# A hybrid encoder block with 16,384 single-neuron experts: the first-table tiles of its dense part shared out anew over the steps and begun three steps earlier

## The reference

```python
def block(xb):                      # 128 tokens
    q = (xb @ w_q).reshape(128, 8, 2, 128)          # 8 heads, two halves
    s1 = einsum('thd,hkd->thk', q[:, :, 0], k1)     # 128 keys each
    s2 = einsum('thd,hkd->thk', q[:, :, 1], k2)
    v1, i1 = top_k(s1, 16);  v2, i2 = top_k(s2, 16)
    cand_s = v1[..., :, None] + v2[..., None, :]
    cand_i = i1[..., :, None] * 128 + i2[..., None, :]
    top_s, pos = top_k(cand_s, 16)                  # 16 experts of 16,384
    idx = take_along_axis(cand_i, pos)
    gate = softmax(top_s)
    u = expert_u[idx];  vv = expert_v[idx]          # a row of 1,024 each
    act = gelu(einsum('td,thkd->thk', xb, u))
    return einsum('thk,thkd->td', gate * act, vv)
x = layer_norm(alpha * x + block(x))
```

## Time and profile before

| | before |
|---|---|
| median of 3 runs | 3006.27 us (3006.0 to 3010.39) |
| the profiled execution | 3014.1 us, its span 3012.3 us |
| TensorE's mean granted clock | 0.921 of full speed |
| TensorE busy | 2616.7 us, 87% |
| VectorE busy | 2327.7 us, 77% |
| ScalarE busy | 1223.7 us, 41% |
| GpSimd busy | 971.8 us, 32% |
| DMA | 1100.76 MB, mean 365 GB/s |

### The profile page before, as it was taken

The page is one execution under the profiler, slowest core; times in us unless marked ns, Lnnn a source line. Parts: engine busy times, 40 slices in busy tenths (PEclk is TensorE's granted clock), DMA queues, the critical chain, the costliest instruction groups (busy, mean ns, idle before and its releaser), DMA issues. The chain is left out here.

```text
span 3012.3 us, 53462 instructions
## 1 busy us (share of the span) xinstructions
PE 2616.7 (87%) x20618; PEld 1518.2 (50%) x20618; DVE 2327.7 (77%) x4875; ACT 1223.7 (41%) x3048; POOL 971.8 (32%) x888
## 2 busy tenths in 40 slices
PE   9899978787887767768888869999998997999997
PEld 7677433232332333323333326666676775766774
DVE  7965577999879899976767867767788884877776
ACT  3254143233345555533333423333244332544454
POOL 0000144444445555544343522223232222211221
PEclk9999999889997777779998989999999999999998
DMA  4113699999999999999999989999999999999995
GB/s 165 63 56 140 240 403 419 413 404 417 412 419 405 420 411 420 419 420 421 421 418 406 419 336 383 397 394 401 400 416 375 397 412 411 386 392 369 410 393 210
DMA packets 175382, 1100.76 MB, mean 365 GB/s; under 512 B 17829, under 2 KB 34341, under 8 KB 52778
## 3 DMA queue, kind: packets, MB, share of 16 engines
q0 software_dynamic: 110592, 805.36, 65.3%
q1 hardware_dynamic: 64554, 292.16, 24.5%
HBM read 1061.79 MB, written 35.65 MB: 364 GB/s over the span
## 5 line engine op out<-in xcount | busy, mean ns | idle before, releaser
L975 POOL DMA_INDIRECT arena_high<-uv_dram,idx_now x768 | 929.3, 1210 | 1665.9 <-PE ps L1258 1525.2
L2430 DVE SCALAR_TENSOR_TENSOR arena_high<-arena_low,arena_high 128x1024 f32<-128x1024 f32 x768 | 922.4, 1223 | 267.4 <-DMA arena_high<-uv_dram,idx_now 261.5
L1258 PE MATMUL ps<-arena_high 32*32 32x512 f32 x12288 | 493.5, 671 | 282.5 <-ACT arena_high L1815 278.1
L1496 PE MATMUL ps<-arena_low 128*128 128x256 f32 x2048 | 463.7, 382 | 0.0
L1496 PEld LDWEIGHTS ps<-arena_low 128*128 128x128 f32 x2048 | 384.0, 190 | 109.4 <-issue 46.0
L1806 ACT ACTIVATE gcol<-hcol 128x2 f32<-128x2 f32 x384 | 77.6, 202 | 824.4 <-DVE arena_high L2430 820.0
L1258 PEld LDWEIGHTS ps<-arena_high 32*32 32x32 f32 x12288 | 94.8, 107 | 481.6 <-ACT arena_high L1815 384.6
L1219 PE MATMUL ps<-arena_low 128*128 128x512 f32 (+1 forms) x512 | 242.0, 616 | 14.3 <-DMA arena_low<-slabs_dram 14.3
L332 PE MATMUL ps<-wv_hi_bytes,w_hi_bytes 128*128 128x512 f32 x512 | 207.6, 406 | 19.4 <-DVE v_lo_bytes L2554 13.1
L1815 ACT ACTIVATE arena_high<-arena_high,wcol 128x32 f32<-128x32 f32 x768 | 204.9, 314 | 12.5
L334 PE MATMUL ps<-wv_hi_bytes,w_lo_bytes 128*128 128x512 f32 x512 | 202.3, 395 | 0.0
(11 more groups left out here) (264 smaller groups left out, 4002.4 us busy)
## 6 DMA issues: line engine op xcount, KB each, us to landing
arena_low<-ut_dram SPq DMA_DIRECT2D x64, 1024.0 KB
arena_high<-vt_dram SPq DMA_DIRECT2D x32, 1024.0 KB, 12.7
arena_low<-vt_dram SPq DMA_DIRECT2D x32, 1024.0 KB
arena_low<-spread_dram SPq DMA_DIRECT2D x32, 512.0 KB
acts_dram<-arena_low SPq DMA_DIRECT2D x14, 1024.0 KB
arena_low<-acts_dram SPq DMA_DIRECT2D x28, 512.0 KB
arena_low<-slabs_dram SPq DMA_DIRECT2D x11, 1152.0 KB
arena_high<-uv_dram,idx_now POOLq DMA_INDIRECT x768
```

Of the source, the lines that this page charges most:

```text
L975: pool.indirect_dma_start(out=ring[:, s % RING, :], out_offset=None, in_=uv_d, in_offset=bass.IndirectOffsetOnAxis(ap=idx_now[:, s:s + 1], ...
L1258: last = nc.tensor.matmul(ps[out:out + QUAD, y_bank(t // PH) + turn, :], diag[rows, s % DIAGS, :], ring[rows, s % RING, cs], start=fresh, ...
L1496: last = nc.tensor.matmul(ps[:, 5 + n % 4 // 2, o:o + 2 * P], u_slot[n % USLOTS][:, k, :], x1T[:, BLK - DENSE:BLK, k, :], start=(k == 0), ...
L2430: last = nc.vector.scalar_tensor_tensor(out=ring[:, s % RING, 0:D], in0=x1[c][:, j, :], scalar=1.0, in1=ring[:, s % RING, 0:D], op0=ALU.mu ...
```

## The change

Four things are altered; what is computed stays the same.

1. *Start of the first table.* It begins three steps earlier (`U0` = 253, step 5 of turn 31). For that slab 12 goes by `beside_u` too: both halves of its queries in bank 4, a quarter in each of steps 1, 2, 4 and 5 of turn 31 (the code shifts them one step ahead of the later slabs' pattern), its scores in step 7, in banks 7 and 4. The first tile now waits for slab 12's scores, not slab 13's. SyncE issues slab 13 before the third tile pair, the one that waits for `y_read`.
2. *Shares.* `u_first` goes by weights: 133 for the steps up to turn 38, 193 for those of turn 39 and after the groups, 95 for the steps with gate groups. Tiles of turns 31 to 43 were 0, 10, 11, 11, 11, 11, 11, 11, 11, 11, 10, 11, 9 and are 3, 11, 10, 11, 10, 11, 10, 11, 15, 8, 8, 12, 8.
3. *Gate groups.* On 18 steps (21, 21, 22 groups in turns 40 to 42 become 24, 29, 11), beginning at G = 321; VectorE builds the one-hot tiles one step ahead in four buffers; in a step TensorE and ScalarE do the groups before the tiles. The picks are still turned round at G = 320.
4. *Second table.* 29 steps in place of 31, from G = 348; 7 steps of experts alone behind it in place of 3. The loads of the gates for the first two chunks are issued at tile 124, ahead of the last pair of first-table loads, not after it. Tiles of turns 43 to 47 were 8, 33, 33, 33, 21 and are 17, 35, 36, 35, 5.

```diff
-U0 = 32 * STEPS
-TAIL = 3
-V_STEPS = 31
+U0 = 32 * STEPS - 3
+TAIL = 7
+V_STEPS = 29
...
-G_STEP0 = PICK0 + DENSE * PH * PICK_PARTS - U0
-G_STEPS = 24
+G_STEP0 = PICK0 + DENSE * PH * PICK_PARTS - U0 + 1
+G_STEPS = 18
+HOTS = 4
+G_BACK = G_STEP0 + G_STEPS + 4
...
+def u_share(s):
+    G = U0 + s
+    if G < PICK0 + 7 * STEPS:
+        return 133
+    return 95 if G_STEP0 <= s < G_STEP0 + G_STEPS else 193
 def u_first(s):
-    return NT * s // U_STEPS
+    return NT * sum(u_share(i) for i in range(s)) // sum(u_share(i) for i in range(U_STEPS))
...
-        hot = at(16, 2, 4, 2 * P)
+        hot = [at(kib, 4, 2 * P) for kib in (16, 20, 28, 32)]
...
         def beside_u(i):
-            return i >= LATE_SLAB + 2
+            return i >= LATE_SLAB + 1
...
             for n in range(NT):
+                if n == USLOTS - 2:
+                    for half in range(2):
+                        load_slab_late(LATE_SLAB + 2, half)
                 if n % 2 == 0:
                     load_u(n // 2)
...
+                if n == u_first(G_BACK) + USLOTS:
+                    for c in range(2):
+                        for part in range(2):
+                            load_g(c, part)
...
-            for c in range(2):
-                for part in range(2):
-                    load_g(c, part)
...
                 if n == 0:
-                    pe.wait_ge(q_ready, 2 * (LATE_SLAB + 2))
-                    pe.wait_ge(score_ready, LATE_SLAB + 2)
+                    pe.wait_ge(x1T_ready, NB)
+                    pe.wait_ge(q_ready, 2 * (LATE_SLAB + 1))
+                    pe.wait_ge(score_ready, LATE_SLAB + 1)
...
-                if s == G_STEP0:
+                if s == G_STEP0 - 1:
                     for j in range(DENSE):
                         turn_picks(j)
-                if 0 <= s < U_STEPS:
-                    for n in range(u_first(s), u_first(s + 1)):
-                        u_tile(n)
                 o = s - G_STEP0
                 if 0 <= o < G_STEPS:
                     for i in range(g_first(o), g_first(o + 1)):
                         g_group(i)
+                if 0 <= s < U_STEPS:
+                    for n in range(u_first(s), u_first(s + 1)):
+                        u_tile(n)
...
-                    for k in {0: (0, 1, 2, 3), 1: (4, 5, 6, 7), 3: (8, 9, 10, 11), 4: (12, 13, 14, 15)}.get(g, ()):
+                    o = g - (1 if i == LATE_SLAB + 1 else 0)
+                    for k in {0: (0, 1, 2, 3), 1: (4, 5, 6, 7), 3: (8, 9, 10, 11), 4: (12, 13, 14, 15)}.get(o, ()):
...
-                if i >= 2:
-                    wait_again(dve, g_psum, i - 1)
+                if i >= HOTS:
+                    wait_again(dve, g_psum, i - HOTS + 1)
...
-                o = s - G_STEP0
+                o = s - G_STEP0 + 1
                 if 0 <= o < G_STEPS:
                     for i in range(g_first(o), g_first(o + 1)):
                         hot_group(i)
```

35 lines of the change are left out of this document (18 added, 17 removed).

## The result

The changed kernel takes 3075.31 us (median of 4 runs, 3073.85 to 3076.1) against 3008.33 for the kernel before beside it (3006.0 to 3013.42): a ratio of 1.022, 95% interval 1.0202 to 1.0237. The profiled execution took 3076.1 us, its span 3074.3, which is 62.0 more than before; forecast was a span of 2988 and a median of 2982, with a range of 2962 to 3004. So 86 us are missing, and one stage holds two thirds of them.

The account below looks back on a forecast made before the run. TensorE was taken to bound turns 33 to 37, VectorE the gate groups, transfers (421 GB/s) the second table. Terms -7.6 - 10.6 + 11.3 - 2.4 - 21 - 9 + 14.5 = -24.8, taken as 24: span 2988, median 2982, range 2962 to 3004.

Parts of the forecast that it names:

- Part 3: Turns 40 to 42, gate groups on 18 steps: VectorE at 9.2 us a step, 227 us against 229.4, 2 earlier.
- Part 4: Turn 42 to the second table's first product: four steps of two tiles plus 4 us, 36.6 us, 21 earlier.
- The tail: Behind the last second-table tile, 7 steps instead of 3: end at +44 us instead of 29.5, 14.5 later.
- Turn 32: Start of the first table: 70.4 us instead of 82.6, with 1.5 us waiting for the pair behind y_read; ends 7.6 earlier.
- 33 to 37: Turns bound by TensorE: three first-table tiles fewer at 3.54 us each, 10.6 us earlier.
- The second table's: Second-table stage: 417 us scaled by bytes per tile, 1.26/1.29, to 408, 9 earlier.
- The two query halves in one bank: Head 12's queries: half 1 waits for ScalarE's copy of half 0; priced at 0, or 0.6 us without cover.
- rival (b): Second-table stage: transfers stop binding, TensorE's 386 us and a ramp remain, 396 for 408; 2970 us, chance 9%.
- The clock: Turns 40 to 42: a clock falling because TensorE idles more would show the forecast wrong; no size given.
- Rival (a): Second-table stage gives nothing back: one more stall of 7 us and the 9 us gone; 2998 us, chance 17%.
- (d): Start of the first table: the pair behind y_read or the slab holds turn 32 as before; 2994 us, chance 7%.
- Rival (c): Turns 40 to 42: gate groups close a loop of TensorE, ScalarE and VectorE; 60 us more, median 3042, chance 7%.

Follow-up runs that it names:

- tiles_first: The changed kernel with TensorE and ScalarE doing first-table tiles ahead of gate groups in a step again, stores unchanged; 3044.71 us, 1.0124 of before.
- groups_24_behind: The changed kernel with the gates' first loads behind the last first-table pair again and groups on 24 steps instead of 18; 3000.87 us, 0.9982 of before.
- store_early: The changed kernel with SyncE issuing each store of gates four tiles earlier, as soon as its chunk is full; 3007.73 us, 1.0008 of before.
- split_gates: store_early with chunk 0's gate loads four tiles earlier and chunk 1's behind the last first-table pair; 3002.25 us, 0.9981 of before.
- tail_3: store_early with 3 steps of experts alone instead of 7 and the second table on 33 steps instead of 29; 3000.42 us, 0.9977 of before.
- groups_24_tail_3: store_early with groups on 24 steps, all first gate loads behind the last first-table pair and 3 steps of experts alone; 2982.81 us, 0.9911 of before.

## Why the prediction was wrong

**Part 3 is the step that failed**, by 58.5 us. The prediction summed VectorE, TensorE and the bytes of the turns with groups and left out SyncE's queue there: from "with 64/18 = 3.56 groups a step is 3.4 + 5.8 = 9.2 us on VectorE" to the 227 no term is for the time at which a store is issued and lands (its bytes are in the 3.5 MB a step). In its place the runs show ScalarE waiting 74.9 us for stores, and 57 us gone from these turns once the stores go out in time. Three of its own facts met in them. Fewer tiles in turns 40 and 41 (8 and 8 instead of 11 and 10) make the pairs' loads rarer, behind which stores stand; groups ahead of tiles put the tile that such a load waits for behind the next chunk's groups; and 18 steps shorten the time until the buffer is wanted. tiles_first and groups_24_behind show what the second and the third are worth; the rarer loads were not run by themselves. The order of SyncE's queue was in plain view, and the prediction looked at it for slab 13 and the gates, not for L857. Without the stores its sum was right: store_early has 228.2 us for its 227. Turn 41 of store_early, as a window, has VectorE busy (the third number) for 77.06 of 78 us, over the 95% that the prediction asked for, though the turn's 79.0 us are 9.9 a step and not 9.2:

```profile
2355.00:2433.00 78.00, 67.50 (x600) 54.82 (x584) 77.06 (x216) 31.34 (x92) 17.84 (x18) 0.96 0.97 395
```

**Part 4 failed too**, by 20.3 us, by an item on the same queue. The time of issue was right (the end of turn 42) and so nearly was the time from issue to use (33 us for 27). What was missed is that the loads' issue holds SyncE for 18.6 us and the last pair for 10.1 more. The trace of before had shown it: there the issue of the four took 12.07 us. Only second-table loads stood behind them, which had time. Half of the 20.3 us came from the late stores: store_early alone has 47.3 us. The other half goes with the split: split_gates has 37.5 us for the 37.1 forecast.

**The tail** was sized at 14.5 us more and cost 19.8, at the prediction's own upper bound (slots freed late). After the end, 16.9 us from the last dots to the last instruction were right; the last dots ended 32 us after the last product instead of 27:

```profile
3025.13 1.22 DVE L2479 SCALAR_TENSOR_TENSOR arena_low<-arena_low,ps 128x1024 f32<-128x1024 f32 x1 [6.21 <-PE ps L344]
...
3056.20 1.23 DVE L2447 SCALAR_TENSOR_TENSOR arena_high<-arena_low,arena_high 128x1024 f32<-128x1024 f32 x1 [1.22 <-DMA arena_high<-uv_dram,idx_now]
```

GpSimd issued its last gather at 3043.70, 19 us after the last product, and the ones before it as the experts freed slots; VectorE, which the experts' dots need, was busy with norms and dots from 3025.1 to 3044.9 without a break. tail_3 shows what the longer tail cost.

**Turn 32** was forecast 2.7 us too short: the wait for the pair behind `y_read` was 3.84 us instead of 1.5, and the tile behind it, at half clock (0.50 granted from 1788 to 1791), took 5.38 instead of 3.54, while the merge took 2.3 instead of 3.8:

```profile
1787.04 5.38 PE L1511 MATMUL ps<-arena_low 128*128 128x256 f32 x16 [3.84 <-DMA arena_low<-ut_dram]
```

**Right were** the turns whose bound the rows of before had shown: 33 to 37 (307.9 for 307.7, the odd ones 60.2 and the even ones 63.7, as said), 38, and 39 (61.9 for 61.8). The second table's 407.2 for 408 is in part luck: five more kernels with the same 29 steps took 408.5 to 417.4 there (tiles_first the most, as long as before with 31 steps), so a gain of 9 us is not safe. The two query halves in one bank cost nothing: TensorE's only waits in turn 31 are 13.7 us for ScalarE's last step before the experts (L1831). That turn is still 2.5 us longer than forecast; its last three steps took 19.4 us for the 19.3 of the sum, so the rest lies before them. Two small slips move nothing: 61.7 less 21 groups at 1.63 leaves 27.5, not 27.2, and by the prediction's own sizes rival (b)'s turn asks for 419 GB/s, not 424. The clock, named as a sign of being wrong, fell as well: 0.86 in turns 40 to 42 with the holes, 0.95 in store_early without them.

Rival (a) did not come in the changed kernel, (b) and (d) not either. Rival (c) is the instructive one. It named the right turns, the right direction and even the sign to look for, VectorE idle before the one-hot tiles, released by the groups' products. The changed kernel's list of VectorE's waits, 2276 to 2560, has it:

```profile
DVE arena_low L2542 <- PE ps L1524: 60.1, 10, 15.8
```

and store_early's, 2276 to 2503, has it no more:

```profile
DVE arena_low L2542 <- PE ps L1524: 0.3, 1, 0.3
```

The stores' place alone was changed between the two, so VectorE's waits were the end of the chain and not its cause: TensorE waited for ScalarE's copy, the copy for a store, the store for SyncE. The prediction gave (c) 7% and 60 us on a chain of engines; the chain that closed ran through a queue and a landing, so that the size nearly fits (58.5 us) is luck.

## What to carry to other kernels

A store that frees a buffer belongs to the path as soon as anything ahead of it in its queue waits: when groups, tiles or steps are re-dealt, list for each DMA what its queue waits for just ahead of it, and on which engine that stands behind what. Ask of each double buffer not only whether its transfer is short enough, but when it is issued. When work is pressed into fewer steps, first the transfers that belong to it have to be issued at the moment of their own readiness. An early load is not free on a queue with a needed load behind it. And before work is pressed into fewer steps, look which engine sets the pace in the steps that it leaves: where that is another one, they give little back.

## What the runs showed of the hardware

The issue of a DMA on SyncE took 0.33 to 0.51 us in most rows, but 7.0 and 10.6 us for the third and fourth load of the gates in a row (0.5 MB each), and 10.1 for the load of 1 MB behind them; two such loads in a row took 0.93 and 0.98 together (split_gates). What makes the later ones long was not taken apart.

The stores of the gates (L867, chunks of 2 MB in one or two transfers) landed 9.8 to 19.2 us after their issue in the changed kernel, 14.2 in the median.

The granted clock was 0.86 on average in turns 40 to 42 of the changed kernel, with TensorE busy for 208 of 284 us, and 0.98 in groups_24_tail_3, with 196 of 218. It changed between two levels, 2.4 and 1.2 GHz. TensorE idled from 2372 to 2390 and then took up groups and a tile; from 2375 to 2395 the clock was at the lower level, and that tile (2393.92) took 4.35 us instead of 3.6:

```profile
2375.00:2395.00 20.00, 4.63 (x19) 4.48 (x20) 4.23 (x13) 2.53 (x8) 0.00 (x0) 0.50 0.61 253
```
